# Three more blocks of gate columns made in attention, and the branches' merge kept in PSUM with release by pairs

## The chip, the cores and the metric

One core of a Trainium2 chip runs the whole kernel, in one launch. The metric is the device time of one execution in microseconds (us). Products run on TensorE (PE in the rows), elementwise work on VectorE (DVE), ScalarE (ACT) and GpSimd (POOL); SyncE (SP) issues the loads.

## The reference

Two networks run one after the other on 256 tokens of width 1024, all in fp32. The first (feed-forward halves, a Fourier and a retention mixer, modulated) is untouched but for code that is written in another way. The second has two layers of this form:

```python
u = rmsnorm(x, ln1_w[l])
proj = u @ w_in[l]
rw = token_shift(proj[..., :RWKV_COLS], rwkv_mu[l])
...
g_a, g_b, g_c = [jax.nn.sigmoid(c) for c in cols[11:14]]
o_a = rwkv7_mixer(...)
o_b = nsa_mixer(...)          # compressed, selected and window attention
o_c = swa_sink_mixer(...)     # window attention with sinks
merged = g_a * (o_a @ w_br_a[l]) + g_b * (o_b @ w_br_b[l]) + g_c * (o_c @ w_br_c[l])
x = x + merged @ w_out[l]
x = x + peer_ffn(rmsnorm(x, ln2_w[l]), ...)
return rmsnorm(x, lnf_w)
```

Each of the three gates has 1024 columns of `w_in`, so 24 tiles of 128.

## The kernel before, in words

**Stages.** The kernel is a list of stages, and every engine goes through them in the same order. A layer of the second network is: norm, ProjectIn (`u @ w_in`), Attention (compressed, selected, window and sink attention), Rwkv, Merge (the three branch projections and the gated sum), Project (`w_out`), norm, and the expert stages.

**Weights.** A block is 1 MB of weights: 2 tiles of 128 output columns by 8 of depth, or one of the like. SyncE loads the blocks into a ring of four slots (L3389), and issues block b when TensorE is done with block b-4. A product in full fp32 is made of rounded halves: ScalarE rounds a block (L241), GpSimd subtracts what rounding left (`leave_rest`, L269), and `product` (L250) makes each 128x128 by 128x256 product of three matmuls (L253 to L255). Both are done for half blocks.

**Gates made ahead.** The last `AHEAD` blocks of `w_in` (L71; 16 gate tiles at 8) are not made in ProjectIn. Each is 16 products from the raw ring block and the unsplit input `input_whole`, one fp32 matmul each (L1663, two records in the trace), and they are spread over attention and Rwkv. The table `ahead_points` (L1608) says how many of them stand at each point: 16 behind the compression's small products ("compressed"), 4 ahead of the turn of each of the units 0 to 7, the rest in Rwkv. They all go to the single PSUM bank 6: after 16, ScalarE copies the bank away (L1677), and the next block waits for that copy (`projection_kept`). The sigmoids come later, in two wide instructions (L1684).

**Attention.** 16 units, in 8 pairs: a pair is one branch (compressed, selected, window, sink) of one half of the tokens, a unit its head group. For a unit, TensorE makes scores (L1812) for a pair at a time; VectorE scales, adds the bias (L1959) and takes the maximum; ScalarE makes four exponentials; TensorE turns the tile (L1825) into banks 4 and 5; ScalarE copies it out (L1895, L1892); the values are summed by L1849. The scores of pair q+2 stand behind the turns of pair q. Ahead of the first scores come the hidden sums of the compression (L1775), its second layer (L1782), two products for Rwkv (L1791), the compressed values (L1795) and the gate products. VectorE prepares the compression's input at the end of ProjectIn (`gather_blocks`, L1930), behind the subtraction of the token shift (L2129), and the next stage begins with L2355.

**Merge.** TensorE makes three branch projections of two blocks each, in the order 0, 1, 2: branches 0 and 2 go to PSUM banks 0 to 3 (two column tiles a bank), branch 1 to banks 4 to 7. VectorE multiplies the whole of branch 0 with its gate into `merged` and branch 1 into `part`, both in SBUF (L2622), and adds them (L2636). For each of the four pairs of tiles of branch 2 it then multiplies (L2622) and adds (L2642); ScalarE rounds the pair, and VectorE subtracts the rounded part one pair later (L2627). The last of these signals the stage's end, for which the output projection waits (`stage_done`, L873). Project uses all eight banks, one for each of 8 output tiles, in blocks of two input tiles.

## Time and profile before

| | |
|---|---|
| Time, median of 3 runs | 4592.27 us (4587.55 to 4604.23) |
| Profiled execution | 4598.86 us, of which the span of the trace is 4597.2 |
| Mean granted clock of TensorE | 0.969 of full speed |
| TensorE busy | 94% of the span |
| GpSimd, ScalarE, VectorE busy | 58%, 41%, 41% |
| Chain that ended last | TensorE 84%, VectorE 8%, ScalarE 3%, GpSimd 2%, DMA 1% |

The rows come from the profiled execution, whose times are us from the start of its span. A matmul's duration is that of its record; matmuls overlap, so a run of them takes less than the sum of its records.

### The profile page before, as it was taken

Reading aid. Unit: us, or ns where it says so; the run is one execution under the profiler, and the core shown is the slowest. Engines: PE = TensorE matmul, PEld = TensorE weight load, DVE = VectorE, ACT = ScalarE, POOL = GpSimd, SP = SyncE. Lnnn points to the kernel's source line nnn. Section 1 sums busy time; section 2 is a strip of 40 time slices with the busy share of each in tenths; the row PEclk is TensorE's granted clock in tenths of the full one; section 3 lists DMA queues with packets and bytes.
Section 4 is the critical chain, followed back from the end, with each engine's and each line's share of the span. In section 5 each row is a group of like instructions: output and inputs, shape, how many; then the busy total and the mean of one; then the engine's idle time right before and its main releaser. Section 6 shows DMA issues by size and latency. Waiting matters only on the chain.

```text
span 4597.2 us, 62851 instructions
## 1 busy us (share of the span) xinstructions
PE 4321.3 (94%) x24310; PEld 3698.4 (80%) x24310; DVE 1871.8 (41%) x3572; ACT 1874.6 (41%) x3042; POOL 2645.1 (58%) x1282
## 2 busy tenths in 40 slices
PE   8999999999999999888989999999878899999998
PEld 5777777878778899877888888887867898888886
DVE  5741376032021421454668322223364678222223
ACT  4423343232133443342333555554451334555554
POOL 3443244444444477640366888887630467888886
PEclk9999999999999999988999999999999999999999
DMA  7643367222222244440243355555430242455554
GB/s 258 220 147 92 108 223 251 98 86 100 88 106 92 87 163 173 153 155 19 74 142 101 137 184 190 186 188 205 165 135 19 83 165 69 165 184 190 187 187 160
DMA packets 109504, 659.25 MB, mean 143 GB/s; under 512 B 11504, under 2 KB 17904, under 8 KB 40048
## 3 DMA queue, kind: packets, MB, share of 16 engines
q1 hardware_dynamic: 99072, 637.22, 39.3%
q10 hardware_dynamic: 10224, 19.11, 1.5%
q8 instruction: 149, 2.44, 0.2%
q14 instruction: 59, 0.48, 0.0%
HBM read 646.84 MB, written 9.44 MB: 143 GB/s over the span
## 4 chain that ended last, share of the span: by engine, by line
PE 84%; DVE 8%; ACT 3%; POOL 2%; DMA 1%; issue 1%; SPq 0%; ACTq 0%; DVEq 0%; POOLq 0%
PE ps L3091 14%; PE ps L253 14%; PE ps L254 13%; PE ps L255 13%; PE ps L3081 9%; PE ps L3082 4%; PE ps L3001 3%; PE ps L2797 3%; POOL ring_rest L269 2%; PE ps L1663 1%; DVE arena L2519 1%; ACT rounded L241 1%; PE ps L2187 1%; PE ps L2205 1%; PE ps L1206 1%
## 5 line engine op out<-in xcount | busy, mean ns | idle before, releaser
L269 POOL TENSOR_TENSOR ring_rest<-ring,rounded 128x1024 fp32r<-128x1024 f32 x960 | 2350.3, 2463 | 1403.1 <-ACT rounded L241 1203.7
L253 PE MATMUL ps<-part,rounded 128*128 128x256 f32 (+1 forms) x3456 | 1185.3, 343 | 81.2 <-POOL ring_rest L269 26.0
L254 PE MATMUL ps<-part,rounded 128*128 128x256 f32 (+1 forms) x3456 | 1175.5, 340 | 0.0
L255 PE MATMUL ps<-part,ring_rest 128*128 128x256 f32 (+1 forms) x3456 | 1174.5, 340 | 0.0
L253 PEld LDWEIGHTS ps<-part,rounded 128*128 128x128 f32 x3456 | 670.5, 194 | 168.6 <-POOL ring_rest L269 25.1
L241 ACT ACTIVATE rounded<-ring 128x1024 fp32r<-128x1024 f32 x496 | 496.7, 1050 | 699.9 <-PE ps L255 691.1
L254 PEld LDWEIGHTS ps<-part,rounded 128*128 128x128 f32 x3456 | 671.0, 194 | 67.4
L255 PEld LDWEIGHTS ps<-part,ring_rest 128*128 128x128 f32 x3456 | 669.9, 194 | 68.1
L3180 ACT ACTIVATE rounded<-ring 128x1024 fp32r<-128x1024 f32 x464 | 490.2, 1057 | 334.6 <-DMA ring<-in_weights 332.5
L3081 PE MATMUL ps<-x_parts,rounded 128*128 128x512 f32 x1728 | 616.9, 397 | 1.5 <-ACTq L3015 1.5
L3091 PE MATMUL ps<-rounded,part 128*128 128x512 f32 x2048 | 592.6, 393 | 16.9 <-POOL ring_rest L269 10.0
L3082 PE MATMUL ps<-x_parts,ring_rest 128*128 128x256 f32 x1728 | 484.6, 280 | 0.0
L3091 PEld LDWEIGHTS ps<-rounded,part 128*128 128x128 f32 x2048 | 368.9, 188 | 99.9 <-POOL ring_rest L269 13.4
L3081 PEld LDWEIGHTS ps<-x_parts,rounded 128*128 128x128 f32 x1728 | 324.6, 188 | 79.5 <-ACTq L3015 1.8
L3211 DVE TENSOR_TENSOR ps<-ps,arena 128x256 f32<-128x256 f32 x216 | 134.9, 624 | 551.0 <-ACT ps L3148 551.0
L3082 PEld LDWEIGHTS ps<-x_parts,ring_rest 128*128 128x128 f32 x1728 | 325.9, 189 | 8.3
L3091 PE MATMUL ps<-ring_rest,part 128*128 128x512 f32 x1024 | 320.6, 395 | 0.0
L443 DVE SCALAR_TENSOR_TENSOR ps<-arena,ps 128x512 f32<-128x512 f32 x392 | 269.2, 747 | 10.0 <-DMA arena<-in_mod_weights 7.8
L929 DVE SCALAR_TENSOR_TENSOR x<-ps,mods,x 128x256 f32<-128x256 f32 x80 | 35.8, 481 | 482.3 <-PE ps L255 482.3
L3091 PEld LDWEIGHTS ps<-ring_rest,part 128*128 128x128 f32 x1024 | 192.1, 188 | 47.3
L824 ACT ACTIVATE arena<-ps 128x512 f32<-128x512 f32 (+1 forms) x88 | 47.9, 544 | 406.9 <-PE ps L255 406.9
L3209 DVE TENSOR_TENSOR ps<-ps,arena 128x256 f32<-128x256 f32 x216 | 93.5, 433 | 238.3 <-ACT arena L3145 238.3
(371 smaller groups left out, 5211.3 us busy)
## 6 DMA issues: line engine op xcount, KB each, us to landing
ring<-in_weights SPq DMA_DIRECT2D x528, 1024.0 KB, 4.8
arena<-in_mod_weights SPq DMA_DIRECT2D x128, 512.0 KB, 4.4
arena<-in_mod_lead SPq DMA_DIRECT2D x8, 1024.0 KB, 18.2
held<-arena ACTq DMA_DIRECT2D x20, 256.0 KB, 5.5
arena<-held SPq DMA_DIRECT2D x20, 256.0 KB, 4.7
arena<-bias_scratch ACTq DMA_DIRECT2D x2, 2048.0 KB, 8.7
bias_scratch<-arena ACTq DMA_DIRECT2D x1, 3072.0 KB, 32.1
x<-in_x SPq DMA_DIRECT2D x1, 2048.0 KB, 10.0
```

The costliest lines, as they stand in the source:

```text
L241: self.nc.scalar.activation(c.rounded[:, s % ROUNDED, half], c.ring[:, slot, half], ACT.Copy)\
L253: mm(out, w[0], a[0], start=start, stop=False)
L254: mm(out, w[0], a[1], start=False, stop=False)
L255: return mm(out, w[1], a[0], start=False, stop=stop)
L269: eng.tensor_tensor(c.ring_rest[:, slot, half], c.ring[:, slot, half], c.rounded[:, (self.s0 + r) % ROUNDED, half].bitcast(F32), ALU.subtr ...
L443: v.scalar_tensor_tensor(bank, self.chunk_row(i, k), self.cond[:, k, stream:stream + 1], bank, ALU.mult, ALU.add)\
L2797: last = nc.tensor.matmul(ps[:, 4 + u % self.AHEAD_BANKS, 0:N], self.chip.ring[:, slot, e * KD + k, :], self.z_whole[:, k, :], start=k == ...
L3001: last = self.nc.tensor.matmul(self.chip.ps[:, n % self.BANKS, i * P:(i + 1) * P], self.hot[:, n % self.BUFS, 0, i], self.hot[:, n % self. ...
L3081: nc.tensor.matmul(c.ps[:, r % 2, :], whi[:, k, :], c.x_parts[:, k, :], start=k == 0, stop=False)
L3082: last = nc.tensor.matmul(c.ps[:, r % 2, 0:N], wlo[:, k, :], self.z[0][:, k, :], start=False, stop=k == KD - 1)
L3091: last = nc.tensor.matmul(self.out(t, i), a, w[:, i * 4 * P:(i + 1) * 4 * P], start=False, stop=end and n == 2)
L3180: self.nc.scalar.activation(c.rounded[:, (self.s0 + r) % ROUNDED, half], c.ring[:, f % RING, half], ACT.Copy)\
```

## The change

It has two parts.

**Gates.** `AHEAD` goes from 8 to 11, so ProjectIn has three blocks less, and 48 more of the gate products (six gate tiles more, 22 in all) are made in attention: 8 at a new point "taps", between the hidden sums and their second layer, 24 instead of 16 at "compressed", and 4 ahead of each of the turns 8 to 15. The number of blocks in a layer, and their slots, stay.

**Merge.** The product of branch 1 stays in its PSUM banks; its sum with branch 0 is `two`, in SBUF. Each pair of tiles of branch 2 is multiplied in place in bank i, and added to `two` with its result in bank 4+i. ScalarE rounds from PSUM, and VectorE's subtraction reads PSUM. Each subtraction signals `input_split`. The projection that follows no longer waits for the stage's end: it starts with the four output tiles whose banks the first two pairs used (0, 1, 4, 5), for two input tiles, then the other four (2, 3, 6, 7), and waits for each bank and each input tile by itself. For the other projections, the order of the steps is written by new functions that give the same order as before.

```diff
-AHEAD = 8
+AHEAD = 11
...
         for j in range(self.blocks - 1):
-            for k in range(2):
-                ready(j, k)
-                first = j == 0 and k == 0
-                order = (self.hidden.output_order() if self.hidden else (*range(4, KD), *range(4))) if first else range(KD)
-                for m in order:
...
-                    out = add(j, k, m, first=first)
+            steps = [(k, m) for k in range(2) for m in range(KD)]
+            if j == 0:
+                steps = self.hidden.first_steps() if self.hidden else UPPER_FIRST
+            begun, known = set(), set()
+            for k, m in steps:
+                if k not in known:
+                    ready(j, k)
+                if self.hidden and j == 0 and m not in begun:
+                    self.hidden.bank_free(pe, m)
+                out = add(j, k, m, first=j == 0 and m not in begun)
+                known.add(k)
+                begun.add(m)
             out.then_inc(c.block_done, 1)
...
-    yield "compressed", 16
+    yield "taps", 8
+    yield "compressed", 24
     for u in range(16):
-        yield ("unit", u), 4 if u < 8 else 0
+        yield ("unit", u), 4
...
             last.then_inc(self.chip.block_done, 1)
+        self.ahead.products(pe, "taps")
         pe.wait_ge(self.hidden.sem, self.hidden.at(1))
...
+    def merged(self, i):
+        return self.chip.ps[:, 4 + i, :]
...
+    def first_steps(self):
+        return [(k, m) for ms in ((0, 1, 4, 5), (2, 3, 6, 7)) for k in range(2) for m in ms]
+
+    def bank_free(self, pe, m):
+        if m < 4:
+            pe.wait_ge(self.merged_ready.sem, self.merged_ready.at(m + 1))
+        else:
+            pe.wait_ge(self.merged_split.sem, self.merged_split.at(m - 3))
+
+    def tile_ready(self, pe, i):
+        pe.wait_ge(self.merged_split.sem, self.merged_split.at(i // 2 + 1))
...
+        def pair(i):
+            bank, tiles = self.chip.ps[:, i, :], slice(2 * i, 2 * i + 2)
+            flat = lambda x: x[:, tiles, :].rearrange("p a n -> p (a n)")
+            link(v.tensor_tensor(bank, bank, flat(self.gates[2]), ALU.mult))
+            v.tensor_tensor(self.merged(i), bank, flat(self.two), ALU.add).then_inc(self.merged_ready.sem, 1)
...
-        rest(3).then_inc(self.chip.stage_done, 1)
+        dve.wait_ge(self.chip.block_done, self.block_count(1))
+        v.tensor_tensor(self.first, outputs(0), self.gates[0], ALU.mult).then_inc(self.used.sem, 1)
+        dve.wait_ge(self.chip.block_done, self.block_count(3))
+        link(v.tensor_tensor(outputs(1), outputs(1), self.gates[1], ALU.mult))
+        v.tensor_tensor(self.two, outputs(1), self.first, ALU.add).then_inc(self.used.sem, 1)
+        dve.wait_ge(self.used.sem, self.used.at(2))
+        for half in range(2):
+            dve.wait_ge(self.chip.block_done, self.block_count(4 + half))
+            for i in (2 * half, 2 * half + 1):
+                pair(i)
+            for i in (2 * half, 2 * half + 1):
+                rest(i)
+        dve.wait_ge(self.merged_split.sem, self.merged_split.at(4))
+        dve.sem_inc(self.chip.stage_done, 1)
```

The first fence is TensorE's order ahead of attention's first scores, in the first of the two layers. Before:

```order
L1775 MATMUL ps<-ring,arena 32x256 x15
L1782 MATMUL ps<-arena 128x32 [waits cmp_hidden]
L1782 MATMUL ps<-arena 128x32 x3
L1791 MATMUL ps<-arena,ring 128x32 [waits block_loaded1,rwkv_sig_a,cmp_hidden_kept]
L1791 MATMUL ps<-arena,ring 128x32
L1795 MATMUL ps<-ring,arena 15x64 x4
L1663 MATMUL ps<-arena,ring 128x256 [waits block_loaded2,input_whole]
L1663 MATMUL ps<-arena,ring 128x256 x15
L1812 MATMUL ps<-arena 128x15 [waits cmp_kept]
```

After (every line from 1609 on has another number, so L1663 is L1660 here, L1782 is L1780):

```order
L1772 MATMUL ps<-ring,arena 32x256 x15
L1660 MATMUL ps<-arena,ring 128x256 [waits block_loaded3,input_whole]
L1660 MATMUL ps<-arena,ring 128x256 x7
L1780 MATMUL ps<-arena 128x32 [waits cmp_hidden]
L1780 MATMUL ps<-arena 128x32 x3
L1789 MATMUL ps<-arena,ring 128x32 [waits block_loaded2,rwkv_sig_a,cmp_hidden_kept]
L1789 MATMUL ps<-arena,ring 128x32
L1793 MATMUL ps<-ring,arena 15x64 x4
L1660 MATMUL ps<-arena,ring 128x256 x8
L1660 MATMUL ps<-arena,ring 128x256 [waits block_loaded0,projection_kept]
L1660 MATMUL ps<-arena,ring 128x256 x15
L1810 MATMUL ps<-arena 128x15 [waits cmp_kept]
```

Eight gate products now stand ahead of the second layer of the compression, 24 behind it, and the last 16 of these have a wait of their own for the emptied bank.

The second fence is TensorE's order in attention's second half, from the scores of pair 6 on. Before:

```order
L1812 MATMUL ps<-arena 128x256 [waits attn_biased]
L1812 MATMUL ps<-arena 128x256 x7
L1849 MATMUL ps<-arena 64x512 [waits sum_kept,attn_turned_kept]
L1849 MATMUL ps<-arena 64x512
L1825 MATMUL ps<-cst,arena 128x128 [waits attn_turned_kept,weighted]
L1825 MATMUL ps<-cst,arena 128x128 x7
L1825 MATMUL ps<-cst,arena 128x128 [waits attn_turned_kept,weighted]
L1825 MATMUL ps<-cst,arena 128x128 x7
```

After:

```order
L1810 MATMUL ps<-arena 128x256 [waits attn_biased]
L1810 MATMUL ps<-arena 128x256 x7
L1847 MATMUL ps<-arena 64x512 [waits sum_kept,attn_turned_kept]
L1847 MATMUL ps<-arena 64x512
L1660 MATMUL ps<-arena,ring 128x256 x4
L1823 MATMUL ps<-cst,arena 128x128 [waits attn_turned_kept,weighted]
L1823 MATMUL ps<-cst,arena 128x128 x7
L1660 MATMUL ps<-arena,ring 128x256 x4
L1823 MATMUL ps<-cst,arena 128x128 [waits attn_turned_kept,weighted]
L1823 MATMUL ps<-cst,arena 128x128 x7
```

Four gate products stand ahead of each turn, behind the scores and the values.

The third fence is VectorE's order in the merge. Before:

```order
L2622 TENSOR_TENSOR arena<-ps,arena 128x2048 [waits block_done,branch_used]
L2636 TENSOR_TENSOR arena<-arena 128x2048 [waits branch_used]
L2622 TENSOR_TENSOR arena<-ps,arena 128x512 [waits block_done,dve_link]
L2642 TENSOR_TENSOR arena<-arena 128x512 [waits dve_link]
L2622 TENSOR_TENSOR arena<-ps,arena 128x512
L2642 TENSOR_TENSOR arena<-arena 128x512 [waits dve_link]
L2627 TENSOR_TENSOR part_76<-arena,part_75 128x512 [waits rounded]
L2622 TENSOR_TENSOR arena<-ps,arena 128x512 [waits block_done]
L2642 TENSOR_TENSOR arena<-arena 128x512 [waits dve_link]
```

After:

```order
L2657 TENSOR_TENSOR ps<-ps,arena 128x2048 [waits block_done]
L2658 TENSOR_TENSOR arena<-ps,arena 128x2048 [waits dve_link]
L2643 TENSOR_TENSOR ps<-ps,arena 128x512 [waits block_done,branch_used]
L2644 TENSOR_TENSOR ps<-ps,arena 128x512 [waits dve_link]
L2643 TENSOR_TENSOR ps<-ps,arena 128x512
L2644 TENSOR_TENSOR ps<-ps,arena 128x512 [waits dve_link]
L2649 TENSOR_TENSOR part_76<-ps,part_75 128x512 [waits rounded] x2
L2643 TENSOR_TENSOR ps<-ps,arena 128x512 [waits block_done]
L2644 TENSOR_TENSOR ps<-ps,arena 128x512 [waits dve_link]
```

The operands of the sums and rests are in PSUM (ps) now, and the rests of two pairs stand together behind the second.

## Rows read from the trace of the kernel before

**Rows 1.** The page, part 1: busy us, share of the span, instructions.

```profile
PE 4321.3 (94%) x24310; PEld 3698.4 (80%) x24310; DVE 1871.8 (41%) x3572; ACT 1874.6 (41%) x3042; POOL 2645.1 (58%) x1282
```

**Rows 2.** Stretches: us; busy PE, PEld, DVE, ACT, POOL; PE's clock; DMA share; GB/s.

```profile
2025.90:2057.10 31.20, 30.14 (x204) 23.24 (x204) 17.59 (x57) 19.95 (x92) 7.11 (x9) 0.95 0.26 95
2057.10:2102.10 45.00, 30.35 (x122) 16.67 (x120) 15.16 (x32) 21.58 (x64) 11.65 (x7) 0.66 0.00 1
2309.80:2336.30 26.50, 26.08 (x192) 25.72 (x192) 2.97 (x7) 8.71 (x14) 14.31 (x6) 0.89 0.35 119
...
3423.80:3464.50 40.70, 25.18 (x117) 14.14 (x116) 14.63 (x30) 21.04 (x64) 11.38 (x7) 0.79 0.00 0
```

**Rows 3.** Timeline of SyncE's queue: start, us, engine, line, [idle before <-releaser].

```profile
1975.85 0.33 SPq L3389 DMA_DIRECT2D ring<-in_weights  x1
...
1993.12 0.33 SPq L3389 DMA_DIRECT2D ring<-in_weights  x1
```

**Rows 4.** Timeline at the end of the input projection, VectorE, then GpSimd.

```profile
1974.43 2.70 DVE L2129 TENSOR_TENSOR x<-x,arena 128x1024 f32<-128x1024 f32 x1
1977.49 5.79 DVE L1930 TENSOR_TENSOR arena<-arena,vec 128x480 f32<-128x480 f32 x2
...
1998.44 0.69 DVE L2355 TENSOR_SCALAR arena<-arena 128x1024 f32<-128x1024 f32 x1 [15.15 <-ACT arena L2274]
...
1977.05 5.43 POOL L269 TENSOR_TENSOR ring_rest<-ring,rounded 128x1024 fp32r<-128x1024 f32 x2 [1.00 <-ACT rounded L241]
```

**Rows 5.** TensorE's timeline before the scores, and L3389's one load issued at 2001.6.

```profile
2010.11 1.91 PE L1782 MATMUL ps<-arena 128*128 128x32 f32 x8 [3.78 <-ACT arena L1870]
...
2014.35 9.34 PE L1663 MATMUL ps<-arena,ring 128*128 128x256 f32 x32
...
DMA to landing us min/median/max: 9.0/9.0/9.0
```

**Rows 6.** TensorE's timeline in attention: second half, the next layer's, and a full-clock stretch.

```profile
2061.35 3.79 PE L1812 MATMUL ps<-arena 64*128 64x256 f32 x16
...
2066.79 1.09 PE L1825 MATMUL ps<-cst,arena 128*128 128x128 f32 x8
2070.81 1.94 PE L1825 MATMUL ps<-cst,arena 128*128 128x128 f32 x8 [2.93 <-ACT arena L1895]
2072.68 3.78 PE L1812 MATMUL ps<-arena 64*128 64x256 f32 x16
...
2090.98 7.71 PE L1849 MATMUL ps<-arena 15*64 15x512 f32 x20
2099.49 1.94 PE L1849 MATMUL ps<-arena 128*64 128x512 f32 x8 [0.79 <-ACT arena L1903]
...
3427.07 2.00 PE L1812 MATMUL ps<-arena 64*128 64x256 f32 x16
...
2221.53 5.34 PE L1663 MATMUL ps<-arena,ring 128*128 128x256 f32 x24
```

**Rows 7.** Timeline of VectorE and ScalarE in attention's second half.

```profile
2065.16 1.23 DVE L1959 SCALAR_TENSOR_TENSOR arena<-ps,arena 128x1024 f32<-128x1024 f32 x1 [4.76 <-PE ps L1812]
...
2069.66 1.01 ACT L1895 ACTIVATE arena<-ps 128x1024 f32<-128x1024 f32 x1
```

**Rows 8.** VectorE's timeline in the merge.

```profile
2286.50 2.29 DVE L2622 TENSOR_TENSOR arena<-ps,arena 128x2048 f32<-128x2048 f32 x1 [3.84 <-PE ps L255]
2288.82 4.34 DVE L2636 TENSOR_TENSOR arena<-arena 128x2048 f32<-128x2048 f32 x1
...
2295.91 0.68 DVE L2622 TENSOR_TENSOR arena<-ps,arena 128x512 f32<-128x512 f32 x1
2296.62 2.19 DVE L2642 TENSOR_TENSOR arena<-arena 128x512 f32<-128x512 f32 x1
...
2307.70 0.69 DVE L2642 TENSOR_TENSOR arena<-arena 128x512 f32<-128x512 f32 x1
```

**Rows 9.** TensorE's first record of the output projection.

```profile
2309.84 0.58 PE L253 MATMUL ps<-part,rounded 128*128 128x256 f32 x1 [11.21 <-DVE part L2627]
```

More of the change, by code:

```diff
@@ L762, in released @@
         pass
-    def output_order(self):
-        return (5, 7, 0, 1, 2, 3, 4, 6) if self.side else (*range(4, KD), *range(4))
-    def turn_side(self, pe):
-        if self.side:
+    def first_steps(self):
+        return [(0, m) for m in (5, 7, 0, 1, 2, 3, 4, 6)] + [(1, m) for m in range(KD)] if self.side else UPPER_FIRST
+    def bank_free(self, pe, m):
+        if m == 0:
+            pe.wait_ge(self.h_ready.sem, self.h_ready.at(KF))
+        if self.side and m == 1:
             self.side.turn(pe, self.side.earlier)
-    def side_banks(self, pe):
-        if self.side:
+        if self.side and m == self.side.TURNED:
             self.side.released(pe)
-    def low_banks(self, pe):
-        pe.wait_ge(self.h_ready.sem, self.h_ready.at(KF))
     def tile_ready(self, pe, i):
@@ L853, in dve @@
             self.side.add(dve, link)
+UPPER_FIRST = [(k, m) for k in range(2) for m in ((*range(4, KD), *range(4)) if k == 0 else range(KD))]
 class Project(Stage):
@@ L1107, in released, with first_steps, bank_free @@
         pe.wait_ge(self.var_in.sem, self.var_in.at(RH))
-    def output_order(self):
-        return *range(4, KD), *range(4)
-    def turn_side(self, pe):
-        pass
-    def side_banks(self, pe):
-        pass
-    def low_banks(self, pe):
+    def first_steps(self):
+        return UPPER_FIRST
+    def bank_free(self, pe, m):
+        if m:
+            return
         pe.wait_ge(self.weighted.sem, self.weighted.at(RH))
@@ L2552, in __init__ @@
         self.gates = [gates[:, KD * b:KD * (b + 1), :] for b in self.ORDER]
-        self.merged, self.part = chip.at(B_BIAS, KD, N), chip.at(B_BIAS + KD * N, KD, N)
+        self.first, self.two = chip.at(B_BIAS, KD, N), chip.at(B_BIAS + KD * N, KD, N)
         self.parts = chip.parts_at(B_BIAS + 2 * KD * N, KD, N), chip.parts_at(B_BIAS, KD, N)
@@ L2559, in __init__ @@
         self.merged_rounded = chip.signals("rounded", 4)
+        self.merged_split = chip.signals("input_split", 4)
     def branch(self, pe, b, j):
@@ L2582, in pe, with released, first_steps, bank_free @@
             self.branch(pe, 2, j)
+    def merged(self, i):
+        return self.chip.ps[:, 4 + i, :]
+    def released(self, pe):
+        pass
+    def first_steps(self):
+        return [(k, m) for ms in ((0, 1, 4, 5), (2, 3, 6, 7)) for k in range(2) for m in ms]
+    def bank_free(self, pe, m):
+        if m < 4:
[4 more added lines that the diff above has]
+        pe.wait_ge(self.merged_split.sem, self.merged_split.at(i // 2 + 1))
     def round_output(self, act, b):
@@ L2596, in act @@
                 self.next.round(act, i // 2)
-            tiles = slice(2 * i, 2 * i + 2)
+            to = self.parts[0][:, 2 * i:2 * i + 2, :].rearrange("p a n -> p (a n)")
             act.wait_ge(self.merged_ready.sem, self.merged_ready.at(i + 1))
-            copy(self.parts[0][:, tiles, :], self.merged[:, tiles, :], ACT.Copy).then_inc(self.merged_rounded.sem, 1)
+            copy(to, self.merged(i), ACT.Copy).then_inc(self.merged_rounded.sem, 1)
     def pool(self, pool, link):
@@ L2618, in dve, with outputs @@
         v = self.nc.vector
-        def product(b, tiles):
-            ps = self.chip.ps[:, 4 * (b % 2):4 * (b % 2) + 4, :].rearrange("p b (m n) -> p (b m) n", n=N)
-            return v.tensor_tensor((self.part if b else self.merged)[:, tiles, :], ps[:, tiles, :], self.gates[b][:, tiles, :], ALU.mult)
+        def outputs(b):
+            return self.chip.ps[:, 4 * (b % 2):4 * (b % 2) + 4, :].rearrange("p b (m n) -> p (b m) n", n=N)
+        def pair(i):
[3 more added lines that the diff above has]
+            v.tensor_tensor(self.merged(i), bank, flat(self.two), ALU.add).then_inc(self.merged_ready.sem, 1)
@@ L2630, in dve @@
         dve.wait_ge(self.chip.stage_done, self.index)
         self.before.before.ahead.gated(dve)
-        for b in range(2):
-            dve.wait_ge(self.chip.block_done, self.block_count(2 * b + 1))
-            product(b, slice(0, KD)).then_inc(self.used.sem, 1)
-            dve.wait_ge(self.used.sem, self.used.at(b + 1))
-        link(v.tensor_tensor(self.merged, self.merged, self.part, ALU.add))
-        for i in range(4):
-            tiles = slice(2 * i, 2 * i + 2)
-            if i % 2 == 0:
-                dve.wait_ge(self.chip.block_done, self.block_count(4 + i // 2))
-            link(product(2, tiles))
-            v.tensor_tensor(self.merged[:, tiles, :], self.merged[:, tiles, :], self.part[:, tiles, :], ALU.add)\
-                .then_inc(self.merged_ready.sem, 1)
-            if i:
-                rest(i - 1)
@@ L3263, in second_network @@
         merge = Merge(chip)
-        stages += [merge, Project(chip, tiles_of(merge.parts), KD, N, kept=kept_input(chip)),
+        stages += [merge, Project(chip, tiles_of(merge.parts), KD, N, hidden=merge, kept=kept_input(chip)),
                    expert_norm(chip, columns(vec, "ln2", layer, KD)),
```

12 lines of the change are left out of this document (3 added, 9 removed).

## The prediction

> **What bounds the kernel now.** The page comes first: TensorE is busy 4321.3 of the 4597.2 us span [rows 1], so only the places where it stands still, runs at its lower clock or does work in a dear form can give time. The change touches each layer of the second network in four places. I read a table of stretches for them, then the timeline of the engine that ends each wait. In the table the reader is to see three kinds of stretch. In the first half of attention (2025.9 to 2057.1) TensorE is busy 30.14 of 31.2 us at a granted clock of 0.95. In the second half (2057.1 to 2102.1) it is busy 30.35 of 45 at 0.66: it waits, and what it does runs mostly at 1.2 instead of 2.4 GHz; in the next layer's second half it is 25.18 of 40.7 at 0.79. The output projection after the merge runs at 0.89 [rows 2]; ahead of it TensorE stood idle for 11.21 us, released by VectorE's last instruction of the merge [rows 9].
>
> Times below are those of the trace's first layer; the second repeats it 1361 to 1362 us later.
>
> **Part 1: three blocks leave the input projection.** Each block is 48 products of rounded halves. The loads that follow the blocks' ends are issued at 1975.85 and 1993.12 [rows 3], three blocks apart: 17.27 us, 5.76 a block and 0.12 a product. TensorE paces them, so 17.3 us go per layer. What is late next? VectorE's key norms do not move, since they hang on blocks 10 to 14: the subtraction of blocks ends at 1977.13 (1974.43 + 2.70) and the gather at 1983.28 [rows 4]. The signal that VectorE needs for attention comes 17.3 us earlier, 1981.1 instead of 1998.44 [rows 4]. If the gather kept its 5.79 us, VectorE would be 2.2 us late. But it ran beside POOL's subtractions for the blocks that leave (1977.05 on) [rows 4], and SBUF-to-SBUF work slows then: the 512-wide add takes 2.19 us beside POOL and 0.69 alone [rows 8]. I take the whole 17.3; bounds 15.1 and 17.3. From there to the first scores all waits are the same as before, 17.3 us earlier, the ring's loads included, for the total of blocks and their slots stay.
>
> **Part 2: 32 products ahead of the first scores instead of 16.** 8 stand before the hidden sums, 24 behind them (order rows of the first fence). In the times of before: the taps need the block that is issued at 2001.6 and lands 9.0 us later, at 2010.6 [rows 5], just when the hidden sums are ready anyhow (2010.11, TensorE having idled 3.78) [rows 5]. So they are not in a gap but ahead of L1782. A product is two records; 24 records at 2.4 GHz take 5.3 us [rows 6], with 0.2 of the last one's tail off 0.43 a product and 1.73 for a group of four; at the lower clock I take twice that. The old 16 took 9.34 us, 0.58 each, the first of them at the lower clock [rows 5]. Low bound, all at 2.4 GHz: taps to 2014.1, hidden chain 2.5 (it was 4.24 from L1782 to L1663), 24 products 10.4, one wait of 0.8 for ScalarE to empty the single PSUM bank between two blocks: 2027.8, against scores at 2025.92 now: +1.9. High bound, all at 1.2 GHz: 6.9 + 4.24 + 20.7 + 0.8 = 32.6, +17.3. I take the taps at 0.74 and the 24 near 0.43, since the taps already put TensorE at steady work earlier than before: taps to 2016.5, chain to 2018.9, products and wait to 2030.1: +4.2, and +3.1 in the other layer. Busier ahead of the scores, the first unit should not fall to the lower clock as it did; I give 0.6 back a layer. Sum +3.0 per layer.
>
> **Part 3: 32 products in attention's second half, four before each unit's turn** (second order fence). Queued behind each are the turn and the next scores. The loop that sets the pace runs from the end of one pair's scores to the next turn: VectorE's shift and maximum, 2 x 1.23, four exponentials of ScalarE, the 2.1 that are left, and its copy of the turned tile, 1.01 [rows 7], with 0.1 between: 5.7 us (2065.13 to 2070.81). TensorE has 1.09 (a turn) and twice 1.73 (the products) to do in it at 2.4 GHz, 4.6 in all, so the products are hidden, while the first half shows that this filling keeps the clock at 0.95 [rows 2]. What it then does on the path gets shorter: scores 3.79 to 2.00, turns 1.94 to 1.09, the last values 7.71 to about 4.9 (20 records at the 0.24 of the 8 in 1.94) [rows 6]. Replaying the loop, the period up to the scores at 2061.35 goes from 10.8 to 9.2 us, the next (to those at 2072.68) from 11.3 to 8.7 [rows 6], and from their end at 2076.46 to 2102.1 from 25.7 to 21.8: -8.1. The second layer is less slow now, 40.7 us for the same stretch [rows 2], and by the same replay ends near the same 36 to 37: -4.7; its first period loses 0.6, as there the four products push a turn. Together -12.8. At the lower clock 8.8 us of work (3.45 + 1.94 + 3.45) would not fit in 5.7; bounds per layer -8.1 and +19 (all at 1.2 GHz: the 30.35 of now, of which some 6 are at 2.4 and would double, and 27.6 for the products, 64 against 45).
>
> ScalarE gets two more 0.6 us copies there and its two gate sigmoids go from 1792 to 2560 elements a partition; the copies stand behind an exponential that ends after them, the sigmoids in a stretch where ScalarE waits for TensorE: nothing, at most 0.6 and 1.4 a layer.
>
> **Part 4: the merge.** VectorE's order is in the third fence. Now: a 2048-wide SBUF add of 4.34, then per pair a product of 0.68 and an add and a rest that take 2.1 to 2.9 beside POOL, 0.69 without; the last comes just ahead of TensorE's start at 2309.84, whose last branch product ended 11.21 earlier, at 2298.6 [rows 8, 9]. After: every sum has one operand in PSUM, which in L2622 costs 0.68 while POOL is at work. The 2048 sum costs 2.29 like the product of that width [rows 8], ready at 2291.1; the first two pairs start with their outputs at 2292.4, are merged at 2293.9 and 2295.3 and split at 2296.1 and 2296.9, all ahead of 2298.6. The last two are merged at 2300.0 and 2301.5, split at 2302.2 and 2303.0. TensorE's 8 steps on the first pairs' banks last from 2298.6 to 2301.5 (24 x 0.12), then it takes banks 2, 3, 6, 7 and waits some 0.5 for the last split. POOL's rests of the first two blocks are there at 2298.5 and 2304.6. So the projection starts at 2298.6 and takes 4 x 5.76 + 0.8 = 23.9 us, to 2322.5, at 2.4 GHz, where now it begins at 2309.84 and ends at 2336.3: -13.8 per layer, 11.2 of idle and 2.6 of lower clock. If an add from PSUM into PSUM cost what the SBUF add costs beside POOL (2.19), each pair would come 1.5 later and ScalarE's and VectorE's chain would hold TensorE for some 6: -7.8. Better than -14.5 it can't be.
>
> The Trainium skill says against this part, "VectorE: DVE Perf Modes", "Rules for kernel authors", that a matmul output on which many operations follow is better copied to SBUF first, and its "The TRN2 errata" gives a PSUM source 62 cycles more of fixed cost. The trace shows no such difference: 0.68 with a PSUM operand, 0.69 with none, at 512 elements [rows 8]. By the rule, an estimate from that page, the nine instructions that newly read PSUM (the wide sum, four sums, four rests) would be 0.065 us longer each, 0.6 a layer; by the rows it is nothing.
>
> **The sum**, on the profiled execution (4598.9 us, span 4597.2): -34.6 + 6.0 - 12.8 - 27.6 = -69.0, 4529.9. The median of the runs is 4592.3, 6.6 lower, so 4523.
>
> **Rivals.**
> 1. *The clock does not come back*: the taps and the 24 run mostly at 1.2 GHz (+8 a layer) and the second half gains nothing. For: granted 0.66 there now, and every period has one gap left. Against: the first half, same pattern, at 0.95. -34.6 + 16 - 27.6 = -46: 4546. Chance 0.14.
> 2. *The merge stays VectorE's*: PSUM-to-PSUM sums slow, or the last split late: -7.8 a layer: 4535. Chance 0.08. That the release by pairs does nothing, the projection starting at the last split (2303.0), costs 4.4 a layer: 4532; it is in the range.
> 3. *Slower than before*: the denser stretch keeps TensorE at 1.2 GHz through all of attention. First half +27 (30.1 us of work, nearly all at 2.4 GHz now), second +19, prelude +17, less 17.3 and 13.8: +32 a layer: 4656. It decides once attention loses over 31.1 us a layer. Only a stretch of dense fp32 products that is granted 0.5 would speak for it; none is in the trace. Chance 0.02.
>
> **Chances.** The forecast 0.76, the rivals 0.14, 0.08, 0.02. The range of 8 in 10, 4508 to 4549, takes in rivals 1 and 2 and, below, a prelude at its low bound, a second half that gains 3 us more a layer and a run 5 us under the median. About 0.5% (23 us) is what a measurement of this kernel can tell from no change. Faster by more: 0.94, within: 0.04, slower by more: 0.02.
>
> **What would show it.** In the changed kernel's profile: input projection 17.3 us shorter, gather near 1.3 us; no idle over 0.5 between the last branch product and the projection, VectorE's sums at 0.69, granted clock 1.0 from the merge to the norm; the second half of attention 37 us long in both layers, clock above 0.9; first scores released by TensorE's own order, not by VectorE. Wrong would be a prelude over 8 us longer, turns still at 1.94, or a second half still over 43 us.

## The result and the profile after

The changed kernel takes 4524.68 us (4522.93 to 4528.14, 4 runs), the kernel before 4594.55 (4587.55 to 4604.23, 4 runs): a ratio of 0.9847, 95% interval 0.9828 to 0.9867, 70 us less. 4523 was forecast. Its profiled execution took 4522.93, with a span of 4521.1, 76.1 less than the span before.

Stretches of the changed kernel, as in [rows 2] (us; busy PE, PEld, DVE, ACT, POOL; PE's clock; DMA share; GB/s), attention's two halves and the output projection, then the next layer's second half:

```profile
2009.50:2039.50 30.00, 28.71 (x205) 22.03 (x204) 17.59 (x57) 21.60 (x94) 7.09 (x9) 1.00 0.31 106
2039.50:2075.80 36.30, 32.57 (x186) 22.49 (x184) 15.16 (x32) 22.54 (x66) 11.64 (x7) 1.00 0.16 59
2268.00:2292.40 24.40, 23.63 (x194) 22.95 (x192) 7.01 (x14) 11.97 (x18) 19.40 (x9) 1.00 0.51 173
3367.60:3403.90 36.30, 32.53 (x186) 22.46 (x184) 15.15 (x31) 22.54 (x66) 11.64 (x7) 1.00 0.16 59
```

The reader is to see the column of the clock: it was 0.95, 0.66, 0.89 and 0.79 in [rows 2], and is 1.00 in these four stretches. In the second half TensorE is busy longer than before (32.57 against 30.35 us of records) in a stretch that is 8.7 us shorter.

TensorE's timeline from the end of the input projection to the first scores, which answers to [rows 5]:

```profile
1983.89 1.96 PE L1772 MATMUL ps<-ring,arena 64*32 64x256 f32 x32 [1.99 <-DMA ring<-in_weights]
1989.99 5.76 PE L1660 MATMUL ps<-arena,ring 128*128 128x256 f32 x16 [4.14 <-DMA ring<-in_weights]
1995.59 0.97 PE L1780 MATMUL ps<-arena 128*128 128x32 f32 x8
1996.93 0.63 PE L1789 MATMUL ps<-arena,ring 128*128 128x32 f32 x4 [0.37 <-ACT arena L1870]
...
1998.04 3.72 PE L1660 MATMUL ps<-arena,ring 128*128 128x256 f32 x16
2002.45 7.17 PE L1660 MATMUL ps<-arena,ring 128*128 128x256 f32 x32 [0.69 <-ACT arena L1674]
2009.55 1.07 PE L1810 MATMUL ps<-arena 64*128 64x15 f32 x16
```

The 8 taps start when their block lands and take 5.76 us, 0.72 each; the 24 behind them take 0.45 each. The taps are the part of the change that did not get the full clock:

```profile
1989.90:1995.60 5.70, 5.61 (x17) 4.65 (x18) 5.67 (x11) 0.98 (x1) 2.48 (x1) 0.62 0.70 292
```

Their clock is 0.62 here (0.68 in the second layer); that of the 24 is 1.00 in both. The scores are released by TensorE's own order, no longer by VectorE.

VectorE's timeline in the merge, which answers to [rows 8]:

```profile
2256.46 2.30 DVE L2657 TENSOR_TENSOR ps<-ps,arena 128x2048 f32<-128x2048 f32 x1 [3.79 <-PE ps L255]
2258.80 2.29 DVE L2658 TENSOR_TENSOR arena<-ps,arena 128x2048 f32<-128x2048 f32 x1
2262.54 0.70 DVE L2643 TENSOR_TENSOR ps<-ps,arena 128x512 f32<-128x512 f32 x1 [1.45 <-PE ps L255]
2263.27 0.70 DVE L2644 TENSOR_TENSOR ps<-ps,arena 128x512 f32<-128x512 f32 x1
...
2265.21 1.45 DVE L2649 TENSOR_TENSOR part<-ps,part 128x512 fp32r<-128x512 f32 x2
2268.23 0.70 DVE L2643 TENSOR_TENSOR ps<-ps,arena 128x512 f32<-128x512 f32 x1 [1.57 <-PE ps L255]
2268.96 0.70 DVE L2644 TENSOR_TENSOR ps<-ps,arena 128x512 f32<-128x512 f32 x1
...
2270.90 1.45 DVE L2649 TENSOR_TENSOR part<-ps,part 128x512 fp32r<-128x512 f32 x2
```

A sum into PSUM takes 0.70 us while GpSimd is at work, where the one in SBUF took 2.06 to 2.19. TensorE's products go on from the branches (at 2268.0) without an idle. The last split ends at 2272.35, 4.4 us behind the last branch product, and holds up one weight load of TensorE:

```profile
2272.40 0.19 PEld L253 LDWEIGHTS ps<-part,rounded 128*128 128x128 f32 x1 [0.35 <-DVE part L2649]
```

The product of that load starts 0.43 us behind the one before it instead of 0.12, so the split costs some 0.3 us. The only other wait of the output projection is one of 0.53 us, at 2286.38, for GpSimd's last rest.

**The ledger.** From the timelines of TensorE (us, layer 1 / layer 2). The input projection goes from its first product to the end of its last one; every other stretch goes on from there to the first record of the next, and the last one ends at the first record of the norm.

| stretch | before | after | forecast | measured |
|---|---|---|---|---|
| input projection | 130.3 / 128.5 | 111.1 / 111.3 | -17.3 | -19.2 / -17.1 |
| its end to the first scores | 32.8 / 32.8 | 36.9 / 37.3 | +4.2 / +3.1 | +4.1 / +4.5 |
| attention, first half | 31.2 / 31.2 | 30.0 / 30.0 | -0.6 | -1.2 / -1.2 |
| attention, second half | 45.0 / 41.3 | 36.3 / 36.3 | -8.1 / -4.7 | -8.7 / -5.0 |
| Rwkv and branch products | 196.3 / 196.2 | 192.2 / 192.2 | 0 | -4.1 / -4.1 |
| idle and output projection | 38.0 / 37.8 | 24.4 / 24.4 | -13.8 | -13.6 / -13.4 |

That is -42.7 and -36.2. The rest of the 76.1 is ahead of, between and behind these stretches, in code that is the same: -1.3 in the first network, and the experts' two stretches 2.1 and 2.0 longer. The -19.2 isn't all of the change either: the first two blocks of the projection, which it leaves alone, took 15.1 us at a clock of 0.81 in layer 1 of before, and 13.9 to 14.0 at 0.88 to 0.89 in the three other layers. Without them the projection lost 18.0 and 17.2.

### The profile page after: what moved, and what is told of

The parts are those of the page before. It is cut to its first block, busy times and chain, and to the rows that moved or that the text cites. A ratio compares the mean times of both kernels' runs of the same rounds, so it can differ in the third digit from the quotient of the medians.

```text
span 4521.1 us, 62629 instructions
## 1 busy us (share of the span) xinstructions
PE 4295.4 (95%) x24214; PEld 3674.7 (81%) x24214; DVE 1835.9 (41%) x3572; ACT 1865.2 (41%) x3030; POOL 2605.7 (58%) x1270
## 4 chain that ended last, share of the span: by engine, by line
PE 87%; DVE 6%; ACT 3%; POOL 2%; DMA 1%; issue 1%; SPq 0%; ACTq 0%; DVEq 0%; POOLq 0%
PE ps L3112 15%; PE ps L253 14%; PE ps L254 13%; PE ps L255 13%; PE ps L3102 9%; PE ps L3103 4%; PE ps L3022 3%; PE ps L2818 3%; PE ps L1660 3%; POOL ring_rest L269 2%; DVE arena L2517 1%; ACT rounded L241 1%; PE ps L2185 1%; PE ps L2203 1%; DMA ring<-in_weights 1%
## 5 line engine op out<-in xcount | busy, mean ns | idle before, releaser
L269 POOL TENSOR_TENSOR ring_rest<-ring,rounded 128x1024 fp32r<-128x1024 f32 x948 | 2310.9, 2451 | 1374.0 <-ACT rounded L241 1171.0
L253 PE MATMUL ps<-part,rounded 128*128 128x512 f32 (+1 forms) x3360 | 1152.6, 343 | 59.3 <-POOL ring_rest L269 26.1
L254 PE MATMUL ps<-part,rounded 128*128 128x512 f32 (+1 forms) x3360 | 1143.0, 340 | 0.0
L255 PE MATMUL ps<-part,ring_rest 128*128 128x512 f32 (+1 forms) x3360 | 1142.2, 340 | 0.0
L253 PEld LDWEIGHTS ps<-part,rounded 128*128 128x128 f32 x3360 | 646.6, 192 | 146.1 <-POOL ring_rest L269 24.6
L241 ACT ACTIVATE rounded<-ring 128x1024 fp32r<-128x1024 f32 x484 | 484.6, 1050 | 672.3 <-PE ps L255 663.5
L255 PEld LDWEIGHTS ps<-part,ring_rest 128*128 128x128 f32 x3360 | 646.3, 192 | 68.5
L254 PEld LDWEIGHTS ps<-part,rounded 128*128 128x128 f32 x3360 | 647.0, 193 | 67.0
L3201 ACT ACTIVATE rounded<-ring 128x1024 fp32r<-128x1024 f32 x464 | 490.2, 1056 | 332.7 <-DMA ring<-in_weights 330.5
L3112 PEld LDWEIGHTS ps<-rounded,part 128*128 128x128 f32 x2048 | 370.5, 189 | 100.3 <-POOL ring_rest L269 13.4
```

What stands on the lines that cost most here:

```text
L241: self.nc.scalar.activation(c.rounded[:, s % ROUNDED, half], c.ring[:, slot, half], ACT.Copy)\
L253: mm(out, w[0], a[0], start=start, stop=False)
L254: mm(out, w[0], a[1], start=False, stop=False)
L255: return mm(out, w[1], a[0], start=False, stop=stop)
L269: eng.tensor_tensor(c.ring_rest[:, slot, half], c.ring[:, slot, half], c.rounded[:, (self.s0 + r) % ROUNDED, half].bitcast(F32), ALU.subtr ...
L3112: last = nc.tensor.matmul(self.out(t, i), a, w[:, i * 4 * P:(i + 1) * 4 * P], start=False, stop=end and n == 2)
```

## The experiments

All on top of the kernel before or the changed one, as said. "Layers" is the time of the two layers from the first product of the input projection to the first record of the norm behind the output projection in the run's trace, without the experts: 941.5 before, 862.5 after (868.3 in a second trace of it). The kernel before was run beside every group of kernels, with medians of 4593.05 to 4597.31; the ratios and the differences of medians below are to the one beside it. For the first four it was 4595.98.

| kernel | median | ratio to before, 95% | layers |
|---|---|---|---|
| gates_only | 4552.08 | 0.9893 to 0.9926 | 894.2 |
| merge_only | 4572.45 | 0.9930 to 0.9963 | 919.4 |
| merge_late | 4584.07 | 0.9962 to 0.9985 | 925.6 |
| release_only | 4589.54 | 0.9976 to 0.9997 | 927.8 |
| no_taps | 4535.59 | 0.9848 to 0.9885 | 875.6 |
| first_half | 4571.31 | 0.9916 to 0.9962 | 917.0 |
| ten | 4539.32 | 0.9859 to 0.9896 | 881.4 |
| after_again | 4530.05 | 0.9842 to 0.9877 | 868.3 |
| shift_1 | 4528.62 | 0.9839 to 0.9872 | 863.3 |
| early_gate | 4527.63 | 0.9835 to 0.9869 | 866.8 |
| early_twelve | 4525.77 | 0.9824 to 0.9861 | 865.2 |
| early_filled | 4520.72 | 0.9814 to 0.9849 | 864.6 |

### The two parts alone

`gates_only` is the kernel before with the two edits of the gates:

```diff
-AHEAD = 8
+AHEAD = 11
-    yield "compressed", 16
+    yield "taps", 8
+    yield "compressed", 24
     for u in range(16):
-        yield ("unit", u), 4 if u < 8 else 0
+        yield ("unit", u), 4
...
+        self.ahead.products(pe, "taps")
```

> Only the first part of the change: 11 gate blocks ahead, placed as in the changed kernel; the merge as before. Theory (the two parts add up, and the denser attention also keeps the clock up in Rwkv, where the changed kernel's trace is 4.0 us a layer shorter than I forecast): per layer -17.3 in the input projection, +4.3 ahead of the scores, -1.2 in attention's first half, -8.7 and -5.0 in the second, -4.0 in Rwkv: -50 in all, near 4543. The forecast's own terms without Rwkv: -41, near 4552. Rival (Rwkv's 4.0 were chance, and the second half owes its clock to nothing here): -34.6 + 8.6 = -26, near 4567. Idle ahead of the output projection stays at 11.2 us.

Measured: 44 us less by the medians, 47.3 in the layers. Ahead of the scores 37.1 and 37.2, halves 29.95 and 36.34, idle ahead of the output projection 11.2: as in the changed kernel. Rwkv takes 195.0, which lies between; so the -50 was too much, and the 4 us of Rwkv don't come from the gates alone.

`merge_only` is the changed kernel with the old gates:

```diff
-AHEAD = 11
+AHEAD = 8
...
-    yield "taps", 8
-    yield "compressed", 24
+    yield "taps", 0
+    yield "compressed", 16
     for u in range(16):
-        yield ("unit", u), 4
+        yield ("unit", u), 4 if u < 8 else 0
```

> Only the second part: the merge through PSUM with release by pairs; 8 gate blocks ahead as before. Theory: 11.5 us of idle and 2 us of lower clock go per layer, -27 in all, near 4566; attention's second half stays at 45 and 41 us with the granted clock of before. Rival (with a less dense attention before it, the projection doesn't get its clock back): -23, near 4571.

Measured: 23.5 less by the medians, 22.1 in the layers. The output projection is 24.42 us with no idle, though attention's second half stays at 45.0 in both layers: the rival on its clock falls. Together the parts give 69.4 us in the layers, the changed kernel 79.0. Of the 9.6 us between, 3.7 are the second half of `merge_only`'s second layer (45.0, where the kernel before has 41.3), 1.9 are that layer's input projection (1.2 of it in the first two blocks, at a lower clock), and 4.9 are in Rwkv (-2.5 and -0.8 alone, -8.2 together). So the parts add up but for Rwkv and for what that one layer did.

### Cheaper sums or earlier release

`merge_late` is `merge_only` with the output projection waiting for the stage's end:

```diff
-        stages += [merge, Project(chip, tiles_of(merge.parts), KD, N, hidden=merge, kept=kept_input(chip)),
+        stages += [merge, Project(chip, tiles_of(merge.parts), KD, N, kept=kept_input(chip)),
```

> The merge through PSUM, but the output projection waits for the stage's end again and takes its tiles in the old order; 8 gate blocks ahead. It tells the cheaper sums from the release. Theory: VectorE's last split ends some 4.4 to 5 us behind the last branch product, so the idle falls from 11.2 to 5 us: -6.5 a layer, and -1 to -2.6 more if the clock holds over 5 us of idle: -13 to -18 in all, near 4578. Rival (the release by pairs is what brings it, the sums' place little): -2 in all, near 4591.

`release_only` has the sums of before in SBUF and in the old order, and waits by bank and tile. Against the kernel before, the new functions are:

```diff
+    def first_steps(self):
+        return UPPER_FIRST
...
+    def bank_free(self, pe, m):
+        if m < 4:
+            pe.wait_ge(self.merged_ready.sem, self.merged_ready.at(m + 1))
...
+    def tile_ready(self, pe, i):
+        pe.wait_ge(self.merged_split.sem, self.merged_split.at(i // 2 + 1))
```

> Release alone: sums stay in SBUF and in the old order of VectorE, but the output projection starts on the first split tiles and waits for each bank and tile; 8 gate blocks ahead. Theory: VectorE's sums beside GpSimd (2.1 to 2.9 us each) still set the end: bank 3 is free at 2308.4 of the old trace, so only the 1.9 us of products on the first tiles come out of the 11.2 of idle: -2 a layer, -4 in all, near 4589. Rival (release is the main thing): over -12 in all, under 4581.

Measured: -11.9 for `merge_late` and -6.4 for `release_only` by the medians. The first record of the output projection in `merge_late`, then in `release_only`:

```profile
2305.29 0.58 PE L253 MATMUL ps<-part,rounded 128*128 128x256 f32 x1 [4.27 <-DVEq L2667]
```

```profile
2294.57 0.55 PE L253 MATMUL ps<-part,rounded 128*128 128x256 f32 x1 [3.10 <-DVE part L2639]
```

The cheaper sums take the idle from 11.2 to 4.3 us. Behind it the clock is still the lower one: this record takes 0.58 us. With release alone TensorE starts after 3.1 us, but stands still for another 2.6 for a sum of VectorE, and its clock from the branches' end to the norm is 0.90. From the last branch product to the end of the output projection it is 38.0 and 37.8 us before, 29.7 and 31.0 in `merge_late`, 33.0 and 33.1 in `release_only`, 24.4 in both layers with the two together. So in these stretches the sums' place is the larger part (-15.1 of the -27.0 in both layers), the release alone brings -9.7, over twice what I expected, and neither rival holds. The medians say less of both, with the same order; they take in the clock's falls elsewhere.

### Where the gate products stand

`first_half` moves the second half's 32 products to the first:

```diff
-        yield ("unit", u), 4
+        yield ("unit", u), 8 if u < 8 else 0
```

> The changed kernel with the 32 products of the second half moved to the first: 8 ahead of each of the turns 0 to 7, none ahead of 8 to 15. Theory (in the second half they fill the waits and hold the clock; in the first there is no wait left to fill): first half +13 to 14 us a layer (32 x 0.43), second half back at 41 to 45 us with a clock of 0.66 to 0.8, +5 to +9, Rwkv loses up to 4: +18 to +27 a layer, near 4570. Rival (the second half's gain came from the clock that the dense prelude set up, not from its own products): second half stays near 36 less the products, under 36: +13 a layer or less, 4550 or under.

Measured: the first half takes 43.0, 13.1 more (32 x 0.41), the second 42.6 and 45.1, Rwkv 195.8 and 195.9, and the median is within 2 us of the forecast. The second half's stretch in the first layer:

```profile
2057.30:2099.90 42.60, 27.01 (x123) 15.37 (x121) 15.15 (x31) 21.49 (x64) 11.64 (x7) 0.76 0.00 1
```

The clock is 0.76 here although the first half before it ran at 1.00. So it is the second half's own products that hold its clock, and 32 products there cost less than nothing, in the first half 13 us. With them the stretch was 36.34 to 36.35 us in every layer of every kernel but one (36.69); without them it was 41.3, 41.6, 42.6, 45.0 or 45.1.

`ten` takes the 16 products ahead of the scores back into the input projection, `no_taps` only moves the taps behind:

```diff
-AHEAD = 11
+AHEAD = 10
-    yield "taps", 8
-    yield "compressed", 24
+    yield "taps", 0
+    yield "compressed", 16
```

> 10 gate blocks ahead: the second half's 32 products stay, the 16 extra ones ahead of the first scores go back to the input projection. Theory: +5.8 a layer there, ahead of the scores -4.1 and -4.5 (as before the change), first half +1.2 by its lower clock: +2.7 a layer, near 4530, with second half still 36.3 us. Rival (the extra products ahead of the scores cost more than the block that they save, since each product takes 0.43 to 0.72 against 0.36 in the projection): -1 or less a layer, under 4523.

```diff
-    yield "taps", 8
-    yield "compressed", 24
+    yield "taps", 0
+    yield "compressed", 32
```

> The changed kernel with the 8 gate products between the hidden sums and their second layer moved behind it (32 at 'compressed', 0 at 'taps'). Theory (the taps are on the path, but they raise the clock for what follows): the hidden chain starts 6.2 us earlier, takes 4.2 instead of 2.3 us and the first 16 products 9.3 instead of 5.6, 0.3 for a missing idle: scores 1 to 1.5 us later per layer, +2 to +3, near 4527. Rival (the taps' 5.8 us at 1.2 GHz are plain loss): the chain and all that follows come at full clock, -2.2 a layer, near 4520. Both are close to what can be told by time, so the profile decides: first scores against the end of the input projection, 36.9 us in the changed kernel.

Measured, to the first scores: `ten` 34.7 and 34.2 (forecast 32.8), first half 32.6 and 31.2, second half 36.3; `no_taps` 38.04 and 38.07, which is the 1 us later that I expected. But the medians are 4539.3 and 4535.6, where 4530 and 4527 were expected, and the layers 19 and 13 us longer than the changed kernel's 862.5. Rwkv has 9.2 of the 19 and 11.3 of the 13: it takes 195.8 and 197.8 in `ten`, and 197.8 twice in `no_taps`, where the changed kernel has 192.2. Rwkv of `no_taps`:

```profile
2079.00:2276.80 197.80, 184.24 (x1360) 170.72 (x1361) 108.22 (x152) 53.69 (x71) 40.45 (x17) 0.97 0.15 54
```

The same stretch of the changed kernel:

```profile
2075.80:2268.00 192.20, 179.41 (x1360) 166.18 (x1361) 106.03 (x152) 53.36 (x71) 40.57 (x17) 0.99 0.15 56
```

1360 matmuls on either side; TensorE's records are 4.8 us longer, at a clock of 0.97 instead of 0.99. In tables of 8 us pieces the clock of the changed kernel falls once in Rwkv (0.79 in the seventh piece), that of `no_taps` three times (0.65 in the seventh, then 0.79 twice).

### Why Rwkv is faster

One more copy on VectorE between the two networks shifts all that follows by its 1.3 us:

```diff
+        link(self.nc.vector.tensor_copy(self.chip.x[:, 0:4, 0:N], self.chip.at(B_U, KD, N)[:, 0:4, :]))
         self.nc.vector.tensor_copy(self.chip.x[:, :, 0:N], self.chip.at(B_U, KD, N)).then_inc(self.chip.stage_done, 1)
```

> The changed kernel with one more VectorE copy of 128x1024 between the two networks (it writes again what the next one writes), 1.2 to 1.3 us on the path, and nothing else. Theory A (how often the clock falls in a stretch such as Rwkv depends on when the stretch comes, not on its instructions): the same instructions take another time in some stretch, as 192.2 becoming 194 to 196 us for Rwkv, or 197.8 as in the kernel without taps; median anywhere from 4523 to 4534. Theory B (the 4 us in Rwkv are caused by what the change put ahead of it): all stretches as in the changed kernel, 192.2 in both layers, 4526.

The changed kernel was run beside it once more:

> The changed kernel once more, as the measure for the runs beside it. 4525, by all theories; its stretches as in its first trace (36.9 and 37.3 us ahead of the scores, 30.0, 36.3, Rwkv with the branch products 192.2), unless the clock's falls come elsewhere.

Measured: Rwkv takes 192.1 to 192.2 in both layers of both, as in the first trace. A shift of 1.3 us doesn't move Rwkv, so theory A is not borne out there. (In `after_again` the stretch ahead of the first layer's scores took 41.2 instead of 36.9 us by a lower clock, and Rwkv was the same.) But theory B isn't shown by it: the two layers of one kernel have the same program, and Rwkv took 195.8 and 197.8 in `ten`, 193.6 and 197.9 in `early_gate`, 194.6 and 192.1 in `early_filled` (the last two are shown below). So the program alone doesn't fix it.

The traces tell one thing more of theory A. The first two blocks of the input projection, which no kernel here changes, take 13.9 to 14.0 us in 17 of the 28 traced layers, and 15.1 to 15.3 at a lower clock in nine. Further on, something is longer in eight of these nine than in the other layer of the same kernel, or of before: the second half 45.0 instead of 41.3 (before, `merge_late`, and both layers of `merge_only`), the stretch ahead of the scores 41.2 and 41.4 instead of 37.2 (`after_again`, `first_half`), 36.8 instead of 33.6 (`early_filled`), 34.2 instead of 32.8 (`early_gate`). The two layers between, with 14.3 and 14.9, are the ones with a second half of 36.69 (`shift_1`) and 41.6 (`release_only`). The second half of `first_half` goes the other way (42.6 there, 45.1 in its other layer). No run tests what brings such a layer about. But a difference of up to 4 us in one layer between two kernels can be of this kind, and so can 3.7 of the 8.7 us that the second half lost in the first layer.

Of Rwkv's 4.1 us, 2.8 lie between `gates_only` and the changed kernel, and begin at one place. In Rwkv's last chunk VectorE multiplies a state in SBUF beside GpSimd's subtraction. VectorE, then GpSimd, in the changed kernel:

```profile
2215.79 2.93 DVE L2482 TENSOR_TENSOR arena<-arena 64x256 f32<-64x256 f32 x2
...
2215.80 2.64 POOL L2622 TENSOR_TENSOR part<-arena,part 128x1024 fp32r<-128x1024 f32 x1
```

And in `gates_only`:

```profile
2216.67 5.16 DVE L2486 TENSOR_TENSOR arena<-arena 64x256 f32<-64x256 f32 x2
...
2216.69 2.37 POOL L2607 TENSOR_TENSOR part<-arena,part 128x1024 fp32r<-128x1024 f32 x1
```

Both engines start within 0.02 us of each other. Each VectorE row is two operations. In the changed kernel the first of them gets through in 0.42 us and GpSimd's is the longer (2.64); in `gates_only` it takes 2.66 and GpSimd's 2.37. It was 0.42 in all six layers that were traced of the changed kernel and its shifted copy, 2.66 to 2.69 in all eighteen of before, `gates_only`, `merge_only`, `merge_late`, `release_only`, `no_taps`, `first_half`, `ten` and `early_twelve`. `early_gate` and `early_filled`, described below, have one layer of each kind. In `gates_only` TensorE then waits 0.83 us for VectorE, besides waits of 2.2 and 0.9 us that follow in both, and the clock falls: the stretch at the first branch products has a clock of 0.83 in `gates_only` (the first row below), of 1.00 in the changed kernel (the second).

```profile
2229.60:2239.80 10.20, 9.32 (x65) 9.16 (x65) 1.38 (x2) 2.32 (x3) 0.55 (x1) 0.83 0.08 13
```

```profile
2227.80:2236.50 8.70, 7.81 (x65) 7.65 (x65) 1.38 (x2) 2.31 (x3) 0.55 (x1) 1.00 0.09 17
```

The same 65 matmuls take 1.5 us more. What decides the race is not settled. Up to there `gates_only` issues the same instructions in the first layer, and in `early_filled` the operation comes 139.9 us behind Rwkv's start in both layers, as in the changed kernel, and takes 2.67 us in the first (Rwkv 194.6) and 0.42 in the second (192.1).

### A better order

TensorE waits 2.0 us for the compression's last block and 4.1 for the first gate block. `early_gate` loads the first gate block before the compression's last one and makes its 16 products there:

```diff
-    yield "taps", 8
-    yield "compressed", 24
+    yield "early", 16
+    yield "taps", 8
+    yield "compressed", 8
...
+            if self.FIRST + j == self.EARLY:
+                self.ahead.products(pe, "early")
```

> The changed kernel with the first gate block loaded ahead of the last block of the compression's weights and made (all 16 products) before it; 8 products of the second at 'taps', 8 behind the second layer of the compression. Same number of products. Theory (TensorE waits 2.0 us for the last compression block and 4.1 to 4.5 for the first gate block, and hidden sums can't be had before 1989.6 of the changed kernel's trace, since ScalarE makes them behind Rwkv's exponentials): the products fill the waits, 5.2 us less, but VectorE's preparation of Rwkv ends at 2005.4, 4.1 us ahead of the scores of now, and bounds it: -4 a layer, -8 in all, near 4517. Rival (the clock's falls in Rwkv, which moved by up to 5.7 us a layer between kernels with the same Rwkv): anything from 4509 to 4528.

Its timeline up to the scores:

```profile
1986.01 8.68 PE L1664 MATMUL ps<-arena,ring 128*128 128x256 f32 x32 [2.34 <-DMA ring<-in_weights]
1994.62 1.09 PE L1779 MATMUL ps<-ring,arena 64*32 64x256 f32 x32
1995.65 3.72 PE L1664 MATMUL ps<-arena,ring 128*128 128x256 f32 x16
...
2001.66 3.72 PE L1664 MATMUL ps<-arena,ring 128*128 128x256 f32 x16
2007.22 1.07 PE L1817 MATMUL ps<-arena 64*128 64x15 f32 x16 [1.84 <-DVE arena L1948]
```

The scores come at 32.8 and 34.2 us behind the input projection, 4.1 and 3.1 earlier, bounded by VectorE as expected. But the median is 4527.63, between the changed kernel's two (4524.68 and 4530.05). The new wait of 1.84 us is followed by a lower clock (31.2 instead of 30.0 in the first half), and Rwkv takes 193.6 and 197.9: gained 7.2, given back 9.5. That all of the 9.5 comes from the new wait isn't shown: the second layer is one of those with slow first blocks (15.3 us).

`early_twelve` has all 12 gate blocks ahead, the last 16 products at the end of Rwkv's first half:

```diff
-AHEAD = 11
+AHEAD = 12
-        yield (t, "outputs"), 0
+        yield (t, "outputs"), 16 if t == 0 else 0
```

> The same, and all 12 gate blocks ahead: the 16 further products stand at Rwkv's 'outputs' of the first half, ahead of a wait of 2.2 us for VectorE. Theory: -5.8 us in the input projection, +6.9 - 2.2 there: -1 a layer more than the kernel with 11, near 4515. Rival (the clock's falls move again, or the single bank's copy comes on the path): between 4510 and 4530.

Measured 4525.77, its layers 865.2: no better than with 11. Rwkv takes 199.1 and 199.2, the 16 further products included.

`early_filled` fills the wait of 1.84 with 4 products taken from ahead of turn 6:

```diff
-    yield "compressed", 8
+    yield "compressed", 12
     for u in range(16):
-        yield ("unit", u), 4
+        yield ("unit", u), 4 if u != 6 else 0
```

> The kernel with the early gate block, with 12 instead of 8 products behind the compression's second layer and none ahead of the turn 6. There VectorE's preparation let TensorE wait 1.8 us before the first scores, and the granted clock was lower behind it. Theory (that wait brought the clock down, and through it the times in the first half and in Rwkv): 32.8 us ahead of the scores without an idle over 0.2, first half 29.95 less 1.7, second half 36.3, Rwkv 192.2 in both layers: -9 to -10 us against the changed kernel, near 4518. Rival (the clock falls in Rwkv anyway, and VectorE's operation beside GpSimd takes 2.7 instead of 0.4 us there): Rwkv 195 to 198, near 4526, the same as the changed kernel.

Measured 4520.72 (4514.70 to 4523.94), the lowest median of all; its interval overlaps that of the changed kernel. Layer 2 went nearly as expected (33.6, 30.2, 36.3, 192.1: 3.5 us less than the changed kernel). Layer 1, whose first blocks were slow, didn't: 36.8 to the scores with a lower clock right behind the input projection (0.62 over 8 us), 31.6 in the first half and 194.6 in Rwkv.

## Why the prediction was right

**Right, term by term.** The input projection (-17.3 against -18.0 and -17.2, without its first two blocks): the three blocks went at TensorE's pace, and nothing of VectorE was late, since the gather fell from 5.79 to 1.83 us (near 1.3 was said) once GpSimd's rests beside it were gone. The second half (-8.1 and -4.7 against -8.7 and -5.0): both layers came to the same 36.3. The merge (-13.8 against -13.6 and -13.4): it waited some 0.3 us for the last split, where 0.5 was said, and 0.53 for GpSimd's last rest.

**Mis-sized, slightly.** Ahead of the scores +3.1 was said for the second layer, and it was +4.5. The taps' block landed 18.0 us behind the input projection there and 17.4 in the first layer, where 17.5 was taken; the taps took 0.69 and 0.72 each (0.74 was said), the 24 behind them 0.45 (0.43). For the 1.1 us less that the second layer was given the working names no row, and both layers before took 32.8; +4.2 for both would have been near. The first half gave back 1.2, twice what I took.

**Missed.** Rwkv, -8.2 in both layers together, was in no term. So the sum was too small: -69.0 against -76.1 in the spans, in which the experts' +4.1, the first network's -1.3 and 1.2 of the first two blocks count too. On the profiled execution 4529.9 was forecast and 4522.9 measured, 7 us too many. The median still came out within 2 us, because the profiled execution of before lay 4.3 us above its median (6.6 was taken) and that of after 1.8 below: by medians it is -69.9. That closeness is luck; what was right is the terms.

**The rivals.** Clock not coming back: no, 1.00 in both halves of attention, in the output projection and over the 24 products; only the taps ran at the lower one (0.62 and 0.68), as their price had it. The merge staying VectorE's: no, 0.70 us a sum into PSUM. Slower: no. The 62 cycles that the prediction quotes from the Trainium skill ("VectorE: DVE Perf Modes", "The TRN2 errata") don't show in these traces: 0.70 us with a PSUM operand, 0.69 with none and GpSimd idle, at 512 elements. Its advice in "Rules for kernel authors", to copy a matmul output to SBUF when many operations follow, would have been the wrong way here: beside GpSimd a sum in SBUF took 2.06 to 2.19 us.

**Open.** What decides between 0.42 and 2.67 us in Rwkv, in which of its short waits the clock falls, and what makes the first blocks of some layers slow. So of Rwkv's 4.1 us a layer, 2.8 begin at one operation, whose cause is open, and 1.3 lie ahead of it and are not traced.

## What to carry to other kernels

Work of TensorE that can stand anywhere belongs into the stretch that waits most often, not where it is dense: 32 products there made it 5 to 9 us shorter and cost 13 us elsewhere. Where VectorE works beside GpSimd, keep one operand of each operation in PSUM: a sum of 512 elements fell from over 2 us to 0.70. After removing a wait, look at the next one behind it: `early_gate` saved 7.2 us ahead of the scores and lost 9.5 behind them, in part at least by a new idle of 1.8. So compare whole layers, not the stretch, and more than one layer.

## What the hardware showed beyond that

The second half of attention without its products has several lengths, from the same instructions: 41.3, 41.6, 45.0 us (42.6 and 45.1 in `first_half`). With its waits filled it is 36.3 us in every traced layer but one. Two engines that start on SBUF within 0.04 us of each other end in one of two ways, 0.42 or 2.67 us for the same 64x256 operation; in twelve of the fourteen traces both layers go the same way, in two one layer goes each way.
